# Modulation weights of a hybrid decoder layer taken in two halves, and two instructions moved

## The reference, cut to what matters

```
mod = silu(c) @ W_ada + b_ada                    # 6 x 1024: shift1, scale1, gate1, shift2, scale2, gate2
h   = rms_norm(x) * (1 + scale1) + shift1
proj = h @ W_in                                  # all branches' input columns
o_a = RG-LRU branch (conv4, block gates, scan)   # "the recurrence"
o_b = RWKV-7 time mixing (16 heads, delta rule)
o_c = sliding-window attention, 4 groups of 4 heads, head-wise norm of q and k
x   = x + gate1 * (gated sum of the three branches) @ W_out
x   = x + gate2 * SwiGLU(rms_norm(x) * (1 + scale2) + shift2)
```

## Time and profile before

| | us |
|---|---|
| median of 3 timed runs | 2896.04 (2893.48 to 2904.6) |
| the profiled execution, its own time | 2904.03 |
| its span | 2902.2 |
| first dense matmul of the opening starts | 50.46 |

### The profile page before, as it was taken

How to read it: one execution, slowest core, us unless ns; L and a number is a source line. 1 busy time by engine, 2 the same in 40 slices (tenths; PEclk the granted TensorE clock), 3 DMA queues, 4 the chain that set the end, 5 groups by cost and what they waited for, 6 DMA issues and landing times.

```text
span 2902.2 us, 60941 instructions
## 1 busy us (share of the span) xinstructions
PE 2824.1 (97%) x25827; PEld 2361.5 (81%) x25827; DVE 1465.3 (50%) x1579; ACT 765.1 (26%) x1107; POOL 775.6 (27%) x510
## 2 busy tenths in 40 slices
PE   4999999999999999999999999999999999999999
PEld 3798979898888888877877777888888888888887
DVE  5745555545464646487774666566654222222223
ACT  4312121313131312145455777011122000000001
POOL 0403030403030312134341112333333333333332
PEclk9999999999999999999999999999999999999999
DMA  5201020202020101133322112465311111111112
GB/s 195 75 28 59 20 64 15 75 4 76 11 69 24 56 25 45 41 126 112 119 81 55 57 45 76 157 209 190 104 44 58 51 43 51 51 45 49 51 46 77
DMA packets 222623, 201.54 MB, mean 69 GB/s; under 512 B 22369, under 2 KB 193467, under 8 KB 222395
## 3 DMA queue, kind: packets, MB, share of 16 engines
q1 hardware_dynamic: 208928, 150.70, 17.2%
q10 hardware_dynamic: 13467, 47.31, 4.6%
HBM read 167.57 MB, written 30.41 MB: 68 GB/s over the span
## 4 chain that ended last, share of the span: by engine, by line
PE 90%; DVE 4%; ACT 3%; issue 2%; DMA 1%; SPq 0%; POOL 0%; ACTq 0%; DVEq 0%; POOLq 0%
PE ps L255 66%; PE ps L891 3%; PE ps L905 3%; PE ps L902 2%; PE ps L869 2%; PE ps L954 1%; PE ps L1091 1%; PE ps L859 1%; PE ps L1116 1%; PE ps L1104 1%; DVE arena L1987 1%; DMA arena<-in_w_ada 1%; PE ps L825 1%; PE ps L911 1%; PE ps L938 1%
## 5 line engine op out<-in xcount | busy, mean ns | idle before, releaser
L255 PE MATMUL ps<-x_hi,w_hi 128*128 128x512 f32 (+1 forms) x2544 | 820.1, 397 | 4.0 <-POOL w_lo L247 1.3
L255 PE MATMUL ps<-x_lo,w_hi 128*128 128x512 f32 (+1 forms) x2544 | 803.9, 391 | 0.0
L255 PE MATMUL ps<-x_hi,w_lo 128*128 128x512 f32 (+1 forms) x2544 | 803.1, 391 | 0.0
L245 POOL CAST w_hi<-w_raw 128x1024 fp32r<-128x1024 f32 (+2 forms) x221 | 211.7, 958 | 1999.5 <-PE ps L255 1596.2
L255 PEld LDWEIGHTS ps<-x_hi,w_hi 128*128 128x128 f32 (+1 forms) x2544 | 471.4, 188 | 119.4 <-issue 20.0
L255 PEld LDWEIGHTS ps<-x_hi,w_lo 128*128 128x128 f32 (+1 forms) x2544 | 478.5, 188 | 103.3
L255 PEld LDWEIGHTS ps<-x_lo,w_hi 128*128 128x128 f32 (+1 forms) x2544 | 478.6, 188 | 99.5
L247 POOL TENSOR_TENSOR w_lo<-w_raw,w_hi 128x1024 fp32r<-128x1024 f32 (+2 forms) x221 | 483.2, 2187 | 17.7
L255 PE MATMUL ps<-hid,w_hi 128*128 128x512 f32 (+1 forms) x928 | 256.5, 395 | 3.8 <-DVE mod L2007 3.0
L2283 DVE TENSOR_TENSOR arena<-ps,arena 128x1024 f32<-128x1024 f32 x21 | 25.7, 1225 | 373.8 <-PE ps L255 373.8
L255 PEld LDWEIGHTS ps<-hid,w_hi 128*128 128x128 f32 (+1 forms) x928 | 170.8, 188 | 46.8 <-issue 13.9
(11 more groups left out here) (289 smaller groups left out, 3443.3 us busy)
## 6 DMA issues: line engine op xcount, KB each, us to landing
w_raw<-in_w_in SPq DMA_DIRECT2D x78, 512.0 KB, 4.0
arena<-in_w_ada SPq DMA_DIRECT2D x48, 512.0 KB, 5.8
w_raw<-in_w_ffn_in SPq DMA_DIRECT2D x44, 512.0 KB, 3.8
arena<-gates_sig ACTq DMA_DIRECT2D x40, 512.0 KB, 4.2
gates_sig<-arena ACTq DMA_DIRECT2D x24, 512.0 KB, 2.6
w_raw<-in_w_ffn_out SPq DMA_DIRECT2D x22, 512.0 KB, 3.6
arena<-in_x SPq DMA_DIRECT2D x16, 512.0 KB, 7.0
y_a<-arena ACTq DMA_DIRECT2D x10, 512.0 KB, 2.6
```

The costliest lines, as they stand in the source:

```text
L245: nc.gpsimd.tensor_copy(hi, raw).then_inc(s_whi, 1)
L255: ins = nc.tensor.matmul(dst[h], wp, xp[h], start=first and m == 0, stop=last and m == 2)
```

## The change

Three edits.

1. **The opening by halves of channels.** Load n now holds 128 rows (n % 8) of half n // 8: 512 shift and the 512 scale columns of the same channels, in packets of 2 KB. Seven parts instead of five, the first of two loads. DVE takes pieces 0 to 7 into accumulator 0, with the reciprocal behind piece 1; PE sums this half (`mod_sums(0, 0)`) before it transposes any x; then half of `mod` is ready. Of the second half, pieces 8 and 9 are multiplied by PE itself (8 matmuls of one column each, `ADA_ON_PE`) and added by DVE from PSUM; pieces 10 to 15 go to DVE, between which the `x_lo` subtractions of blocks 0 to 2 stand; PE sums them (`mod_sums(1, 4)`) in block k = 2 of its loop. Scaling and shifting out of PSUM moves from DVE to ACT (Identity with scale and bias).
2. **The recurrence:** `later_ada_add(g, 0)` stands ahead of `recur(g, 1)`.
3. **Attention:** `square(nx - 1, 1)` stands ahead of `exps(tick)`.

```diff
-        ADA_ACC0, ADA_OUT0 = ADA0, 3
-
-        ADA_PARTS = [(0, 5), (5, 9), (9, 13), (13, 15), (15, 16)]
+        ADA_ON_PE = (8, 9)
+        ADA_ACC0, ADA_OUT0 = ADA0 - len(ADA_ON_PE), 2 + len(ADA_ON_PE)
+
+        ADA_PARTS = [(0, 2), (2, 5), (5, 8), (8, 10), (10, 12), (12, 14), (14, 16)]
         s_ada = [sem(f"ada_weights_loaded_{k}") for k in range(len(ADA_PARTS))]
 
-        ADA_COLS = [(0, 8), (8, 10), (10, 16)]
+
+        def ada_part(n):
+
+            return next((k, n1 - n0) for k, (n0, n1) in enumerate(ADA_PARTS) if n0 <= n < n1)
+
+        def mod_half(half):
+
+
+            return mod[:, 0:2 * KT].rearrange("p (o k) -> p o k", o=2)[:, :, half * KT // 2:(half + 1) * KT // 2]
...
@@ -540,8 +549,9 @@
                 for n in range(n0, n1):
                     if n >= ADA_SLOTS:
                         sp.wait_ge(ada_acc, upto(n - ADA_SLOTS + 1))
-                    src = w_ada[n // 2 * P:(n // 2 + 1) * P, n % 2 * 1024:(n % 2 + 1) * 1024]
-                    sp.dma_start(ada_w0[:, n % ADA_SLOTS, :], src).then_inc(s_ada[part], 16)
+                    half, row = n // KT, n % KT
+                    src = w_ada[row * P:(row + 1) * P, 0:2048].rearrange("p (o n) -> p o n", o=2)[:, :, half * 512:(half + 1) * 512]
+                    sp.dma_start(halves(ada_w0[:, n % ADA_SLOTS, :]), src).then_inc(s_ada[part], 16)
             load_block(sp, Block("lora", 2), cols(w_in, COL_LORA + 2 * P, 32), 32)
             load_gains(sp)
 
@@ -760,27 +770,41 @@
                     ins = pe.transpose(ps[:, 4 + 2 * (k % 2) + t // 4, (t % 4) * P:(t % 4 + 1) * P], xs[:, t, k * P:(k + 1) * P], ident)
                 ins.then_inc(h_pe, 1)
 
+            def mod_sums(half, bank):
+                pe.wait_ge(ada_acc, upto(KT if half == 0 else ADA_ACC0))
+                for c in range(KT):
+                    ins = mm(ps[:, bank, c:c + 1], ada_acc0[:, half, c * P:(c + 1) * P], ones[:, 0:1], start=True, stop=True)
+                ins.then_inc(ada_pe, 1)
+
+
+            mod_sums(0, 0)
             pe.wait_ge(p0_act, upto(18))
             for k in range(2):
                 transpose_x(k)
-            for part, (c0, c1) in enumerate(ADA_COLS):
-                half = c0 // 8
-                pe.wait_ge(ada_acc, upto(ADA0 - 1 + half))
-                for c in range(c0, c1):
-                    ins = mm(ps[:, part, c:c + 1], ada_acc0[:, half, c % 8 * P:(c % 8 + 1) * P], ones[:, 0:1], start=True, stop=True)
+            for q, n in enumerate(ADA_ON_PE):
+                part, count = ada_part(n)
+                pe.wait_ge(s_ada[part], 16 * count)
+                for c in range(KT):
+                    ins = mm(ps[:, 1 + q, c:c + 1], ada_w0[:, n % ADA_SLOTS, c * P:(c + 1) * P], mod[:, 48 + n % KT:49 + n % KT], start=True, stop=True)
                 ins.then_inc(ada_pe, 1)
 
 
             lora = [Block("lora", c) for c in range(2)]
             for blk in lora:
                 pe.wait_ge(s_wsplit, upto(blk.before + 1))
-            pe.wait_ge(ada_out, upto(3))
+            pe.wait_ge(ada_out, upto(1 + len(ADA_ON_PE)))
             for k in range(KT):
                 if k + 2 < KT:
                     pe.wait_ge(h_tmp, upto(k + 1))
-                    transpose_x(k + 2)
+                    if k == 2:
+                        mod_sums(1, 4)
+                    else:
+                        transpose_x(k + 2)
                 pe.wait_ge(h_lo, upto(k + 1))
                 for blk in lora:
+                    if k == 2 and blk is lora[1]:
+                        pe.wait_ge(ada_out, upto(ADA_OUT0))
+                        transpose_x(k + 2)
                     w = [t[:, blk.slot, k * P:(k + 1) * P] for t in (w_hi, w_lo)]
                     x = [[t[:, k, h * 512:(h + 1) * 512] for h in range(2)] for t in (x_hi, x_lo)]
                     ins = three_passes([ps[:, 2 * blk.slot + h, :] for h in range(2)], w, x, k == 0, k == KT - 1)
@@ -1343,6 +1367,11 @@
             act.wait_ge(lam_s, upto(2))
             fn(rate2, rate, ACT.Exp, scale=-1.0).then_inc(p0_act, 1)
             for k in range(KT):
+                act.wait_ge(h_pe, upto(k + 1))
+                act.wait_ge(ada_out, upto(1 if k < KT // 2 else ADA_OUT0))
+                if k >= 2:
+                    act.wait_ge(h_lo, upto(k - 1))
+                fn(halves(h_tmpb[:, k % 2, :]), pair_of(2 + k % 2), ACT.Identity, scale=mod[:, MOD_SC1 + k:MOD_SC1 + k + 1], bias=mod[:, MOD_SH1 + k:MOD_SH1 + k + 1]).then_inc(h_tmp, 1)
                 act.wait_ge(h_tmp, upto(k + 1))
                 fn(x_hi[:, k, :], h_tmpb[:, k % 2, :], ACT.Copy).then_inc(h_hi, 1)
 
@@ -1602,10 +1631,10 @@
                     copy_part(EARLY - 1, 1)
                 if tick in Y_TICKS:
                     high_y(*Y_TICKS[tick])
+                if nx <= GROUPS and j == 0:
+                    square(nx - 1, 1)
                 if tick < ALL:
                     exps(tick)
-                if nx <= GROUPS and j == 0:
-                    square(nx - 1, 1)
                 if 0 <= tick - 2 < ALL:
                     probs_copy(tick - 2)
                 if nx <= GROUPS and j == 1:
@@ -1748,46 +1777,55 @@
             dve.wait_ge(lam_s, upto(2))
 
             dve.wait_ge(p0_act, upto(1))
-            for part, (n0, n1) in enumerate(ADA_PARTS):
-                for n in range(n0, n1):
-                    c_k, acc = mod[:, 48 + n // 2:49 + n // 2], ada_acc0[:, n % 2, :]
-                    if n == n0:
-                        dve.wait_ge(s_ada[part], 16 * (n1 - n0))
-                    if n < 2:
-                        ins = v.tensor_scalar(acc, ada_w0[:, n % ADA_SLOTS, :], c_k, None, ALU.mult)
-                    else:
-                        dve.wait_ge(ada_acc, upto(n - 1))
-                        ins = v.scalar_tensor_tensor(acc, ada_w0[:, n % ADA_SLOTS, :], c_k, acc, ALU.mult, ALU.add)
-                    ins.then_inc(ada_acc, 1)
-                if part == 0:
-                    dve.wait_ge(p0_act, upto(10))
-                    step(v.reciprocal(rstd, rstd))
-
-            def ada_add(part):
-
-                c0, c1 = ADA_COLS[part]
-                dve.wait_ge(ada_pe, upto(part + 1))
-                v.tensor_tensor(mod[:, c0:c1], ps[:, part, c0:c1], mod[:, c0:c1], ALU.add).then_inc(ada_out, 1)
-
-            ada_add(0)
-            ada_add(1)
-            dve.wait_ge(ada_out, upto(2))
-
-            def modulate(k):
-                dve.wait_ge(h_pe, upto(k + 1))
-                if k >= 2:
-                    dve.wait_ge(h_lo, upto(k - 1))
-                v.tensor_scalar(halves(h_tmpb[:, k % 2, :]), pair_of(2 + k % 2), mod[:, MOD_SC1 + k:MOD_SC1 + k + 1], mod[:, MOD_SH1 + k:MOD_SH1 + k + 1],
-                                ALU.mult, ALU.add).then_inc(h_tmp, 1)
-            modulate(0)
-            ada_add(2)
-            for k in range(KT):
-                if k + 1 < KT:
-                    if k == 1:
-                        dve.wait_ge(ada_out, upto(3))
-                    modulate(k + 1)
+            def ada_piece(n):
+
+                c_k, acc, first = mod[:, 48 + n % KT:49 + n % KT], ada_acc0[:, n // KT, :], (0, KT + len(ADA_ON_PE))
+                done = n if n < KT else n - len(ADA_ON_PE)
+                part, count = ada_part(n)
+                dve.wait_ge(s_ada[part], 16 * count)
+                if n in first:
+                    ins = v.tensor_scalar(acc, ada_w0[:, n % ADA_SLOTS, :], c_k, None, ALU.mult)
+                else:
+                    dve.wait_ge(ada_acc, upto(done))
+                    ins = v.scalar_tensor_tensor(acc, ada_w0[:, n % ADA_SLOTS, :], c_k, acc, ALU.mult, ALU.add)
+                ins.then_inc(ada_acc, 1)
+
+            added = [0]
+
+            def ada_add(half, bank):
+
+                dve.wait_ge(ada_pe, upto(added[0] + 1))
+                if half == 1:
+                    dve.wait_ge(ada_out, upto(added[0]))
+                v.tensor_tensor(mod_half(half), ps[:, bank, 0:KT].rearrange("p (o k) -> p o k", o=2), mod_half(half), ALU.add).then_inc(ada_out, 1)
+                added[0] += 1
+
+            def h_low(k):
+
                 dve.wait_ge(h_hi, upto(k + 1))
                 v.tensor_tensor(x_lo[:, k, :], h_tmpb[:, k % 2, :], x_hi[:, k, :].bitcast(F32), ALU.subtract).then_inc(h_lo, 1)
+
+            ada_piece(0)
+            ada_piece(1)
+            dve.wait_ge(p0_act, upto(10))
+            step(v.reciprocal(rstd, rstd))
+            for n in range(2, KT):
+                ada_piece(n)
+            ada_add(0, 0)
+            ada_piece(10)
+            for q in range(len(ADA_ON_PE)):
+                ada_add(1, 1 + q)
+            ada_piece(11)
+            h_low(0)
+            ada_piece(12)
+            ada_piece(13)
+            h_low(1)
+            ada_piece(14)
+            ada_piece(15)
+            h_low(2)
+            ada_add(1, 4)
+            for k in range(3, KT):
+                h_low(k)
 
 
             e, z = rate2, small[:, 66:66 + LRU_T]
@@ -2059,9 +2097,9 @@
```

(4 more changed lines are left out.)

## The result

The changed kernel is slower by a little: median 2903.36 us (2898.33 to 2907.86, 20 runs) against 2897.65 us (2892.04 to 2904.6, 20 runs) of the kernel before on the same chip, ratio 1.0018, 95% interval 1.0012 to 1.0024. That is 5.7 us more, where 9 us less (2887) was predicted. Its profiled execution took 2901.53 us, 2.5 less than the profiled one of before, which lies near the top of its range; so the two traces show where time moved, and the medians by how much.

What follows compares the result with a forecast made beforehand. TensorE was taken as the bound, busy 2824.1 of 2902.2 us. Opening 0, recurrence 2.9, attention 5.3 and 1.7 sum to 9.9 us off the profiled execution; 9 off the median 2896.04 gives 2887, range 2878 to 2896.

Steps and rivals of the forecast that it cites:

- The opening: Start of the kernel up to block 0 and the second sums: net 0, outer bounds 6.4 us gained to 4.3 lost.
- the two near cases: Opening, products of pieces 8 and 9 quick or slow: dense start 47.1 or 50.2, net 1.6 us gained or 1.5 lost.
- The rule of the Trainium skill: Opening: TensorE starts throttled, so first sums take 3.4 us; by the printed clock 1.84, and 1.6 more gained.
- The recurrence: later_ada_add ahead of recur: TensorE's wait for it goes in two turns, 2.9 us off, between 0 and 3.0.
- Attention: Square ahead of exps: 5.3 us off at the first tick, 1.7 in the fourth group, from waits and low clock.
- The sum of these: Opening, recurrence and attention: 0 + 2.9 + 5.3 + 1.7 = 9.9 us off the profiled execution.
- that the clock would follow: Attention's low-clock stretches go with the waits; rival, they turn up elsewhere: 4.3 off, 2892, chance 0.20.
- Everything between these places is TensorE back to back: Whole kernel: a microsecond taken from a TensorE wait reaches the end, unless a later wait takes it back.
- the products of pieces 8 and 9, 32 instructions: Opening, on TensorE after the 16 transposes: 3.7 us at the quick rate or 6.8 at the slow one.
- Taken back: Rival: DVE and ACT chains in recurrence and attention take gains back; only first tick's 1.89 stays, 2894, chance 0.08.
- the loads: Rival: opening's half-row 2 KB packets at half pace, 2.6 us a piece, become the bound: 2898, chance 0.04.
- 50.5 of them or nearly so: TensorE's idle time: of 78.1 us, this much was put ahead of its first dense matmul.

Runs made afterwards that it cites:

- orders_only: The kernel before with both reorders (square before exps, later_ada_add before recur) and the old opening: 2888.12 us.
- before_p65: The kernel before with 65 TensorE semaphore increments that nobody waits for, behind the parameters' transposes: 15.9 us slower than the kernel before.
- after_pos: The kernel after with 191 TensorE semaphore increments that nobody waits for, in idle stretches of the opening (65 + 191 = 256): 2889.17 us.
- orders_p72: Both reorders on the old opening, with 72 TensorE semaphore increments that nobody waits for behind the parameters' transposes: 2918.62 us.

## Why the prediction was wrong

- **The opening (0; right, in part by luck).** Reciprocal 25.52 (25.5 to 25.7 forecast), sums at 34.72 and 3.58 us (33.6 and 3.4), 16 transposes 3.47 (3.4), products of pieces 8 and 9 3.85: the quick of the two near cases (3.7). Dense start 47.90 (47.1 or 50.2). Block 0 came 0.4 longer. But the two near cases are not alternatives of which one is true: both happen, in the old opening as in the new. The prediction compared both with the quick outcome of the old one, 50.46, since its one trace had that; `orders_only`, the same opening, starts dense work at 53.68. By the start of the loop the new opening is 0.7 us ahead of the old one among the quick profiles and 0.3 behind among the slow ones, on the average, so 0 stands.
- **The clock at the start.** The rule of the Trainium skill that I weighed against the printed clock ("TensorE: Matmul & The Clock Gate", Part 1: the default state is throttled) held: TensorE's first sums ran at 0.22 us each. The printed 1.00 of the earlier trace rows was no reading of the clock: in that trace its record begins at 42.97.
- **The recurrence (-2.9; mechanism right).** The wait is gone; TensorE gains 1.7 us at each of its two places in the traces. Alone the move measured -4.8, interval 0.9977 to 0.9995, or 1.4 to 6.7 us.
- **Attention (-5.3 and -1.7; mechanism right).** Both waits and both low-clock stretches went, and the traces give back 5.3 us at the first tick and 1.8 in the fourth group. Alone it measured -9.6.
- **The sum of these** was 9.9 us off; the same two orders on the old opening measured 12.3. What I doubted most, that the clock would follow, was not where it failed. Nor was it a merit that the time stayed within 0.5%, to which I gave 0.84: about 12 us less and 16 more, a term that the prediction lacks, happened to cancel nearly.
- **The step that failed** is "Everything between these places is TensorE back to back, so a microsecond taken from one of its waits reaches the end" together with "the products of pieces 8 and 9, 32 instructions". I costed these by their time in the opening and left out that they are also code ahead of a loop: that they move it was put at nothing, without a reason. The missing term is +15.9 (by `before_p65`) or 7 x (142.1 to 142.66 - 140.03) = 14.5 to 18.4. In the profile of after it shows as seven pauses at the loop's top, 1.37 us in the second turn, where before has none. With it: 2897.65 - 12.3 + 15.9 = 2901.3, and 2903.36 was measured. Which edges in the turn's middle make up the rest of the term stays open.
- **No rival had it.** "Taken back" pointed at DVE and ACT, "the loads" at packets of data. The profile of before held a sign of it: 3.7 us in six waits on "issue" at line 938, in the turns, and a queue named "instruction" whose 16 KB packets stand at the loop's top. It could have raised the question of position, but not told which positions are bad. It also shows that TensorE is not back to back between the places of the diff.
- **Two slips of reading.** Of the 78.1 us without work not "50.5 of them or nearly so" lie ahead of the first dense matmul but 39.5, since TensorE works for 11 us there; the other 38.6 lie further on. And pieces 5 to 7 end at 33.3 by the prediction's own terms, not 33.6. Neither moves the result.

## What to carry to other kernels

Instructions that an edit adds or removes on TensorE also move every loop behind them; on the other engines nothing was tried. Where a loop's body runs close to the pace of the instruction fetch, here small matmuls with a weight load each, a version should be compared with its rival at the same position (filler in idle time up to the same place within 256, as in `after_pos`), or a gain of 12 us can be read as a loss of 6. A wait on "issue" that comes once per turn, just behind the jump and not in the first turn, is the sign to look for. And one trace of an opening is one of its outcomes: before a difference of 2 or 3 us is put down to an edit, look whether the kernel alone has it too.

## What the hardware showed that I had not expected

- Behind the backward jump TensorE's next block lands late: over three turns each of `before_p65` and `orders_p72` the paused instruction starts 1.21 to 1.43 us after the second packet has landed, and that packet starts 3.1 to 4.1 us after the one before. In the kernel before the second packet of turn 2 starts 3.8 us after the first, and nothing pauses: the position at which it is needed, not the fetch, is what changes.
- Moving the loop by 7 instructions (65 to 72) cost 9.6 us (11.7 by the distances from before), moving it by 7 x 8 more (to 128) gave 26.6 back (25.8).
- The Trainium skill, "Advanced Engine Details and Errata" (ISA Cache), says "Cache line size: 16KB → 256 instructions". The packets (16,384 bytes), the 252 to 261 recorded instructions between two of them and the period of 256 (`after_pos`) agree.
